# Stick-breaking prompt attention: the suffix sums from one float32 product to two products of rounded parts

## The chip, the cores and the metric

The kernel runs on one core of a Trainium2 chip. TensorE (PE in the rows, its weight loads PEld) does matrix products into the accumulation memory PSUM, VectorE (DVE) does elementwise work, ScalarE (ACT) evaluates functions such as Exp and Ln from tables that it must load first, GpSimd (POOL) and SyncE (SP) issue transfers. Each engine works through its own list of instructions in order and waits on semaphores that the others raise. The metric is the device time of one execution in microseconds (us); lower is better.

## The reference

The program is one layer of a decoder: projections, stick-breaking attention and dilated-window attention for a prompt of 512 positions and for 8 sampled sequences, an output projection, and a feed-forward part with product-key experts. The change touches one piece: the stick-breaking attention of the prompt, for 8 heads.

```python
def stick_breaking_weights(z, mask):
    log_keep = jnp.where(mask, jax.nn.log_sigmoid(-z), 0.0)
    later = lax.cumsum(log_keep, axis=z.ndim - 1, reverse=True) - log_keep
    return jnp.where(mask, jnp.exp(jax.nn.log_sigmoid(z) + later), 0.0)
...
z = jnp.einsum('bqhd,bkhd->bhqk', qi, k) * scale + b
mask = kpos[None, :] < qpos[:, None]
w = stick_breaking_weights(z, mask)
return jnp.einsum('bhqk,bkhd->bqhd', w.astype(v.dtype), v)
```

Since log_sigmoid(-z) is minus softplus(z), the weight of key s for query t is the exponential of z minus the sum of softplus(z) over the keys from s up to the query. So each head needs a suffix sum over keys of the softplus of its logits.

## The kernel before

Keys lie on the 128 partitions, in four blocks (KB = 4). Block kb has its logits for the queries from its own block on, 512, 384, 256 and 128 columns, and the four pieces stand side by side in one tile of WIDE = 1280 columns. Per head h the stage does this:

- **Scores, TensorE** (`scores`, L596 and L598): four products of keys and queries and four that add the mask, into PSUM banks 0 to 2. They wait for the logits of the head before, which empties those banks.
- **Logits, VectorE** (`logits`, L671): scale and bias, PSUM to `sb_z`, three tiles in turn.
- **Log part, ScalarE** (`log_part`, L643 to L645): Abs, Exp of its negative, Ln of one plus that, into `sb_e`; the Ln (and later the Exp again) needs a table load in front of it.
- **Softplus, VectorE** (`softplus`, L680): max(z, 0) plus the log part, into `sb_p`, two tiles in turn. It raises `sb_softplus`.
- **Sums, TensorE** (L624 and L627): for each block one product with a lower triangle of ones (`tri`) and one with a full square of ones (`ones`) for every later block, into PSUM banks 3 to 5. Ten products of 128 to 512 columns, 2560 columns together, all in float32. They raise `sb_sums`.
- **Exponents, VectorE** (L689): z minus the sums, in place in `sb_z`, raising `sb_exponents`.
- **Weights, ScalarE** (L658): Exp in place, after a table load; and `out` (L649) copies the result of the head before.
- **Weigh, TensorE** (`weigh`, L609): ten products of weights and values.

The order on each engine is written out by hand. TensorE: scores of head h+1, sums of h, weigh of h-1. ScalarE: log part of h+1, weights of h, out of h-1. VectorE: logits of h+1, exponents of h, softplus of h+1:

```python
logits(0)
softplus(0)
for h in range(H):
    if h + 1 < H:
        logits(h + 1)
    dve.wait_ge(sem("sb_sums"), h + 1)
    dve.tensor_tensor(sb_z[h % 3], sb_z[h % 3], bank(3, 3)[:, 0:WIDE], ALU.subtract)\
        .then_inc(sem("sb_exponents"), 1)
    if h + 1 < H:
        softplus(h + 1)
```

In the trace a float32 product stands as two matmul records with a weight load each. Elsewhere in the program (the projections at L405, the experts at L2065) a float32 operand is kept as two parts of type float32r, a rounded one and the rest, and the products of the parts are added; a float32r product stands as one record. `own_steps` gives an engine a counting semaphore of its own; `link` raises it on an instruction and waits for it, so that the next instruction may read what this one wrote, and `do` raises it without waiting.

The dilated-window attention (L710 to L820) follows on the same engines, and the sampled sequences come after it, behind a barrier of all engines.

Of the kernel before, what the change touches and what calls it, by code (L numbers as in the profile page):

```python
# [26 lines left out]
F32R = mybir.dt.float32r  # L27
# [3 lines left out]
ALU = mybir.AluOpType  # L31
# [3 lines left out]
P = 128  # L35
# [41 lines left out]
ALL_COLUMNS = 52992  # L77
# [88 lines left out]
def build(nc, x_prompt, x_sample, cache_k_sb, cache_v_sb, page_table, state_k_win, state_v_win,  # L166
# [4 lines left out]
    with ExitStack() as ctx:  # L171
# [20 lines left out]
        def sem(name):  # L192
            name = AGAIN.get(name, name)
            if name not in made:
                made[name] = ctx.enter_context(nc.semaphore(name))
            return made[name]
# [4 lines left out]
        def take_in(stack, name, cols):  # L201

            era_tensor[0] = stack.enter_context(nc.sbuf_tensor(name, [P, cols], F32)), cols, place[0]
# [6 lines left out]
        def take(cols, at=None):  # L210

            if at is not None:
                place[0] = at
            o = place[0]
            place[0] = o + cols
            if place[0] <= KEPT:
                return kept[:, o:o + cols]
            tensor, size, base = era_tensor[0]
            assert o >= base and place[0] <= base + size, (o, place[0], base, size)
            return tensor[:, o - base:o - base + cols]  # L220

        def bank(b, n=1):
            return psum[:, b * BANK:(b + n) * BANK]
# [4 lines left out]
        ident, tri, ones, diag, iota = (sq[:, i * P:(i + 1) * P] for i in range(5))  # L228
# [11 lines left out]
        SAMPLE = place[0]  # L240
        assert SAMPLE == KEPT + ATTENTION
        work_era = ExitStack()
# [30 lines left out]
        def part(engine):  # L273
            return programs[engine].append
        steps = {}

        def own_steps(eng, name):

            if name not in steps:
                steps[name] = Steps(eng, sem(f"{name}_step"))  # L280
            return steps[name]
# [33 lines left out]
        @part("sp")  # L315
        def _(sp):
            sp.dma_start(sq, square).then_inc(sem("square_in"), 16)
            for t in range(4):
                sp.dma_start(x_nat[:, t, :], x_rows[:, t, :]).then_inc(sem(X_IN[t]), 16)
            sp.wait_ge(sem("tail_cleared"), 1)  # L320
            sp.dma_start(x_nat[0:NS, 4, :], xs_rows).then_inc(sem("small_in"), 16)
            sp.dma_start(cos_sb, cosine).then_inc(sem("angles_in"), 16)
            sp.dma_start(sin_sb, sine).then_inc(sem("angles_in"), 16)
            sp.dma_start(pages_sb[:, :], page_table.rearrange("b j -> (b j)").rearrange("(o n) -> o n", o=1))\
              .then_inc(sem("pages_in"), 16)
            for g in range(NG_IN):
                for e in range(2):
                    if g >= 1:
                        sp.wait_ge(sem("w_low"), 2 * (g - 1) + e + 1)
                    sp.dma_start(w_sb[e], w_in_g[2 * COLUMN[GROUPS[g // 2]] + g % 2, e]).then_inc(sem(f"w_in_{e}"), 16)  # L330
# [218 lines left out]
        KB = SEQ // P  # L549
        AT = (0, 512, 1024, 896)  # L550
        WIDE = 1280
        work_era.close()
        place[0] = SAMPLE
        take_in(work_era, "prompt_attention", ALL_COLUMNS - SAMPLE)
        place[0] = WORK
        sb_z = [take(WIDE) for _ in range(3)]
        sb_e = [take(WIDE) for _ in range(2)]
        sb_p = [take(WIDE) for _ in range(2)]
        o_nat = take(4 * D).rearrange("p (t d) -> p t d", t=4)
        counts = take(4 * SEQ).rearrange("p (t k) -> p t k", t=4)  # L560
        bias = small[:, 0:8]
        bias_ht = small[:, 8:40].rearrange("p (h t) -> p h t", h=H)
# [10 lines left out]
        def region(kb):  # L573
            return slice(AT[kb], AT[kb] + SEQ - kb * P)
# [14 lines left out]
        @part("pe")  # L589
        def _(pe):  # L590
            def scores(h):
                if h >= 1:
                    pe.wait_ge(sem("sb_logits"), h)
                for kb in range(KB):
                    r = region(kb)
                    pe.matmul(psum[:, r], lhsT=k_t["sb"][:, h // 2, kb * P:(kb + 1) * P],  # L596
                              rhs=q_z["sb"][:, h, kb * P:SEQ], start=True, stop=False)
                    last = pe.matmul(psum[:, r.start:r.start + P], lhsT=ident, rhs=diag, start=False, stop=True)  # L598
                last.then_inc(sem("sb_scores"), 1)

            def weigh(h):
                pe.wait_ge(sem("sb_weights"), h + 1)
                if h >= 2:
                    pe.wait_ge(sem("sb_out_copied"), h - 1)
                out = bank(6 + h % 2)
                for qb in range(KB):
                    for kb in range(qb + 1):
                        a = AT[kb] + (qb - kb) * P
                        last = pe.matmul(out[:, qb * HD:(qb + 1) * HD], lhsT=sb_z[h % 3][:, a:a + P],  # L609
                                         rhs=v_n["sb"][:, kb, h * HD:(h + 1) * HD], start=(kb == 0), stop=(kb == qb))  # L610
                last.then_inc(sem("sb_out"), 1)


            scores(0)
            for h in range(H):
                if h + 1 < H:
                    scores(h + 1)
                pe.wait_ge(sem("sb_softplus"), h + 1)
                if h >= 1:
                    pe.wait_ge(sem("sb_exponents"), h)  # L620
                sp_h = sb_p[h % 2]
                for kb in range(KB):
                    r = region(kb)
                    last = pe.matmul(bank(3, 3)[:, r], lhsT=tri, rhs=sp_h[:, r], start=True, stop=(kb == KB - 1))  # L624
                    for later in range(kb + 1, KB):
                        a = r.start + (later - kb) * P
                        last = pe.matmul(bank(3, 3)[:, a:r.stop], lhsT=ones, rhs=sp_h[:, region(later)],  # L627
                                         start=False, stop=(later == KB - 1))
                last.then_inc(sem("sb_sums"), 1)
                if h >= 1:  # L630
                    weigh(h - 1)
            weigh(H - 1)
# [29 lines left out]

        @part("dve")
        def _(dve):
            dve.wait_ge(sem("counts_in"), 2 * 16)

            def logits(h):
                dve.wait_ge(sem("sb_scores"), h + 1)
                if h >= 3:
                    dve.wait_ge(sem("sb_out"), h - 2)  # L670
                dve.tensor_scalar(sb_z[h % 3], psum[:, 0:WIDE], SCALE, bias[:, h:h + 1], ALU.mult, ALU.add)\  # L671
                    .then_inc(sem("sb_logits"), 1)

            def softplus(h):

                dve.wait_ge(sem("sb_log"), h + 1)
                dve.wait_ge(sem("sb_logits"), h + 1)
                if h >= 2:
                    dve.wait_ge(sem("sb_sums"), h - 1)
                dve.scalar_tensor_tensor(sb_p[h % 2], sb_z[h % 3], 0.0, sb_e[h % 2], ALU.max, ALU.add)\  # L680
                    .then_inc(sem("sb_softplus"), 1)

            logits(0)
            softplus(0)
            for h in range(H):
# [7 lines that stand above are left out]
# [1673 lines left out]
```

## Time and profile before

| | us |
|---|---|
| median of 3 runs (2473.87 to 2479.03) | 2478.3 |
| the profiled execution, whole | 2474.16 |
| span of its trace | 2472.3 |
| TensorE busy | 2304.7 (93%) |
| VectorE busy | 1549.5 (63%) |
| ScalarE busy | 942.2 (38%) |
| the 8 heads of the stage, first logits to last exponents | 210.94 to 293.32 |

Busy time is the union of an engine's instructions on the span; the span starts with the first instruction that the profiler saw. The stage that the change touches takes about 82 us of the 2472.3, so a number for the whole kernel says little of it: it is read from windows and single rows of that stage.

### The profile page before, as it was taken

The page shows a single profiled execution, that of the slowest core. Times are in us where ns is not written, and L with a number is a line of the kernel's source. Part 1 is how long each engine was busy: PE and PEld are TensorE (multiplying, and loading weights), DVE is VectorE, ACT ScalarE, POOL GpSimd, SP SyncE. Part 2 cuts the span into 40 slices and gives each one's busy share as a digit, 9 for nine tenths or more (in the row PEclk, how much of TensorE's full clock was granted, in tenths as well). Part 3 has the DMA queues.
Part 4 walks back from the last instruction along what each step waited for, and adds up shares of the span by engine and source line. Part 5 has one row for each costly group of instructions (what it writes and reads, how often), then busy time and mean ns, then how long its engine had stood idle before and what let it go on. Part 6 is the DMA issues. An engine that isn't in the chain of part 4 may idle for free.

```text
span 2472.3 us, 37860 instructions
## 1 busy us (share of the span) xinstructions
PE 2304.7 (93%) x12921; PEld 1901.2 (77%) x12921; DVE 1549.5 (63%) x3167; ACT 942.2 (38%) x1432; POOL 393.3 (16%) x370
## 2 busy tenths in 40 slices
PE   7998988998999798999899889999999999999996
PEld 7997765666566446985577688999989899999895
DVE  4352331333444434678998778777777777777777
ACT  3225542444444512223355633333333333333332
POOL 0001000000000000000000044333333333333320
PEclk9999987889999898999999999999999999999998
DMA  4226977877766621203254699999999999999982
GB/s 130 87 88 224 332 237 271 275 263 263 267 207 209 196 66 37 83 21 106 92 197 178 243 333 342 317 313 315 314 313 311 316 315 311 312 313 313 311 294 78
DMA packets 224111, 568.20 MB, mean 230 GB/s; under 512 B 18065, under 2 KB 96466, under 8 KB 221330
## 3 DMA queue, kind: packets, MB, share of 16 engines
q1 hardware_dynamic: 174994, 327.75, 40.2%
q0 software_dynamic: 49024, 239.23, 27.6%
q8 instruction: 56, 0.92, 0.1%
q14 instruction: 37, 0.30, 0.0%
HBM read 528.24 MB, written 105.12 MB: 256 GB/s over the span
## 4 chain that ended last, share of the span: by engine, by line
PE 79%; DVE 8%; DMA 4%; ACT 3%; SPq 3%; issue 2%; POOL 0%; ACTq 0%; DVEq 0%
PE psum L2065 20%; PE psum L2056 16%; PE psum L405 7%; PE psum L1560 5%; PE psum L1839 5%; PE psum L2046 3%; DMA sample<-in_cache_v_sb_dram 3%; PE psum L1862 3%; PE psum L1420 3%; PE psum L1001 3%; PE psum L1055 2%; PE psum L991 2%; PE psum L1073 2%; PE psum L1023 1%; SPq L926 1%
## 5 line engine op out<-in xcount | busy, mean ns | idle before, releaser
L2065 PE MATMUL psum<-expert_parts 128*128 128x512 f32 x2304 | 550.3, 394 | 0.8 <-DVE expert_parts L2184 0.8
L2065 PEld LDWEIGHTS psum<-expert_parts 128*128 128x128 f32 x2304 | 426.7, 188 | 87.3 <-DVE expert_parts L2184 1.8
L2056 PE MATMUL psum<-h_parts,expert_parts 128*128 128x384 f32 x2304 | 444.5, 341 | 2.9 <-DVE expert_parts L2179 1.5
L2056 PEld LDWEIGHTS psum<-h_parts,expert_parts 128*128 128x128 f32 x2304 | 403.0, 189 | 10.9 <-issue 1.8
L2126 ACT ACTIVATE expert_parts<-peer 128x1024 fp32r<-128x1024 f32 x128 | 135.8, 1061 | 358.9 <-PE psum L2065 332.8
L2179 DVE TENSOR_TENSOR expert_parts<-psum,expert_parts 128x512 fp32r<-128x512 f32 x192 | 132.8, 692 | 147.2 <-ACT expert_parts L2120 147.2
L2222 DVE SCALAR_TENSOR_TENSOR kept<-experts,kept 128x1024 f32<-128x1024 f32 x160 | 205.0, 1281 | 8.3 <-DMA experts<-in_peer_v_dram,kept 3.0
L2031 POOL DMA_INDIRECT experts<-in_peer_v_dram,kept x160 | 192.6, 1204 | 70.5 <-issue 47.5
L1839 PE MATMUL psum<-h_whole,gate_table 128*128 128x384 f32 x512 | 180.6, 497 | 10.5 <-ACT gate_table L1891 10.5
L1331 DVE TENSOR_TENSOR sample_parts<-sample,sample_parts 128x512 fp32r<-128x512 f32 x128 | 85.5, 690 | 166.9 <-ACT sample_parts L1184 166.5
L405 PE MATMUL psum<-projection_parts 128*128 128x256 f32 (+1 forms) x1440 | 174.5, 283 | 3.8 <-DVE projection_parts L511 3.8
L405 PEld LDWEIGHTS psum<-projection_parts 128*128 128x128 f32 (+1 forms) x1440 | 170.6, 175 | 6.0 <-issue 3.9
L2120 ACT ACTIVATE expert_parts<-psum 128x512 fp32r<-128x512 f32 x192 | 114.8, 598 | 149.1 <-PE psum L2046 142.5
L2184 DVE TENSOR_TENSOR expert_parts<-peer,expert_parts 128x1024 fp32r<-128x1024 f32 x128 | 155.9, 1218 | 0.0
L1839 PEld LDWEIGHTS psum<-h_whole,gate_table 128*128 128x128 f32 x512 | 93.8, 193 | 67.5 <-issue 18.1
L2026 POOL DMA_INDIRECT experts<-in_peer_u_dram,kept x96 | 95.3, 992 | 314.4 <-DVE experts L2206 180.2
L1160 ACT ACTIVATE sample<-psum 128x512 f32<-128x512 f32 x128 | 75.8, 593 | 164.4 <-PE psum L991 164.4
L2026 POOL DMA_INDIRECT peer<-in_peer_u_dram,kept x62 | 79.7, 1285 | 361.9 <-DVE peer L2206 356.6
L1001 PEld LDWEIGHTS psum<-attention,sample 128*128 128x128 f32 x1024 | 134.7, 204 | 1.6 <-issue 0.8
L2046 PE MATMUL psum<-kept,peer 128*128 128x128 f32 x768 | 115.7, 273 | 16.1 <-DVE expert_parts L2179 15.7
L1001 PE MATMUL psum<-attention,sample 128*128 (+1 forms) x1024 | 130.5, 254 | 0.0
L1023 PE MATMUL psum<-sample_parts 128*64 128x512 f32 x272 | 96.4, 482 | 25.0 <-DVE sample_parts L1331 24.2
(281 smaller groups left out, 3287.1 us busy)
## 6 DMA issues: line engine op xcount, KB each, us to landing
peer<-in_peer_v_dram SPq DMA_DIRECT2D x128, 512.0 KB, 5.0
peer<-in_peer_u_dram SPq DMA_DIRECT2D x96, 512.0 KB, 5.4
sample<-in_cache_k_sb_dram SPq DMA_DIRECT2D x128, 256.0 KB, 3.9
sample<-in_cache_v_sb_dram SPq DMA_DIRECT2D x128, 256.0 KB, 3.0
out_dram<-in_state_k_win_dram POOLq DMA_DIRECT2D x8, 4088.0 KB, 54.4
out_dram<-in_state_v_win_dram POOLq DMA_DIRECT2D x8, 4088.0 KB, 41.2
gates_dram<-gate_table SPq DMA_DIRECT2D x12, 2048.0 KB, 7.3
experts<-gates_dram SPq DMA_DIRECT2D x32, 768.0 KB, 6.8
```

Of the source, the lines that this page charges most:

```text
L405: last = pe.matmul(bank(u % 4)[0:r, 0:WC], lhsT=x_r[:, x, k, t * P:t * P + r], rhs=w_in_r[g % 2][:, y, k, :], start=(n == 1), stop=(n == 3 ...
L1001: last = pe.matmul(bank(2)[:, c:c + 8].rearrange("p (e t) -> p e t", e=2), lhsT=k_turned[j % 2][:, pair, :], rhs=q_s["sb"][:, 2 * pair:2 * ...
L1839: last = pe.matmul(bank(6)[:, 0:ND], lhsT=early_t[e % 2][:, k, :], rhs=h1_f[:, k, :], start=(k == 0), stop=(k == KD - 1))
L2026: pool.indirect_dma_start(out=u_rows[p], out_offset=None, in_=peer_u, in_offset=index(q, p))\
L2031: pool.indirect_dma_start(out=v_rows[p], out_offset=None, in_=peer_v, in_offset=index(q - 1, p))\
L2046: last = pe.transpose(bank(7)[:, k % 4 * P:(k % 4 + 1) * P], u_sb[s][:, k * P:(k + 1) * P], ident)
L2056: last = pe.matmul(bank(6)[:, 0:ND], lhsT=u_t[s][:, a, k, :], rhs=h1_r[:, b, k, 0:ND], start=(k == 0 and n == 0), stop=(k == KD - 1 and n ...
L2065: last = pe.matmul(bank(2 * t + half), lhsT=weight[s][:, a, t * P:(t + 1) * P], rhs=v_r[s][:, b, half * 512:(half + 1) * 512], start=(firs ...
L2126: act.activation(v_r[s][:, 0, :], v_sb[s], ACT.Copy).then_inc(sem("v_high"), 1)
L2179: dve.tensor_tensor(u_t[s][:, 1, ks, :], bank(7).rearrange("p (k j) -> p k j", k=4), u_t[s][:, 0, ks, :], ALU.subtract).then_inc(sem("u_lo ...
L2184: dve.tensor_tensor(v_r[s][:, 1, :], v_sb[s], v_r[s][:, 0, :], ALU.subtract).then_inc(sem("v_low"), 1)
L2222: dve.scalar_tensor_tensor(y, v_rows[p], dots_act[:, p:p + 1], y, ALU.mult, ALU.add).then_inc(sem("added"), 1)
```

## The change

The softplus of a head is still made in `sb_p`, but then split on VectorE into a rounded part (`tensor_copy` into a float32r tile) and what the rounding left (`tensor_tensor` subtract). The ten products per head become twenty, in float32r, a pair of parts for each. `tri` and `ones` are copied once into float32r tiles. The order of logits, exponents and softplus on VectorE is that of before. The memory for the parts, 4 x 1280 + 2 x 128 columns, is taken from the end of the stage's area.

```diff
+        SUMS_R = 4 * WIDE + 2 * P
+        take_in(work_era, "prompt_attention", ALL_COLUMNS - SAMPLE - SUMS_R)
+        sums_tensor = work_era.enter_context(nc.sbuf_tensor("sums_parts", [P, SUMS_R], F32R))
...
+        sp_r = [sums_tensor[:, 2 * e * WIDE:2 * (e + 1) * WIDE].rearrange("p (x n) -> p x n", x=2) for e in range(2)]
+        tri_r, ones_r = (sums_tensor[:, 4 * WIDE + e * P:4 * WIDE + (e + 1) * P] for e in range(2))
...
-                sp_h = sb_p[h % 2]
                 for kb in range(KB):
                     r = region(kb)
-                    last = pe.matmul(bank(3, 3)[:, r], lhsT=tri, rhs=sp_h[:, r], start=True, stop=(kb == KB - 1))
+                    for x in range(2):
+                        last = pe.matmul(bank(3, 3)[:, r], lhsT=tri_r, rhs=sp_r[h % 2][:, x, r], start=(x == 0),
+                                         stop=(kb == KB - 1 and x == 1))
                     for later in range(kb + 1, KB):
                         a = r.start + (later - kb) * P
-                        last = pe.matmul(bank(3, 3)[:, a:r.stop], lhsT=ones, rhs=sp_h[:, region(later)],
-                                         start=False, stop=(later == KB - 1))
+                        for x in range(2):
+                            last = pe.matmul(bank(3, 3)[:, a:r.stop], lhsT=ones_r, rhs=sp_r[h % 2][:, x, region(later)],
+                                             start=False, stop=(later == KB - 1 and x == 1))
...
+            st = own_steps(dve, "dve")
             dve.wait_ge(sem("counts_in"), 2 * 16)
...
-                dve.scalar_tensor_tensor(sb_p[h % 2], sb_z[h % 3], 0.0, sb_e[h % 2], ALU.max, ALU.add)\
+                st.link(dve.scalar_tensor_tensor(sb_p[h % 2], sb_z[h % 3], 0.0, sb_e[h % 2], ALU.max, ALU.add))
+                st.link(dve.tensor_copy(sp_r[h % 2][:, 0, :], sb_p[h % 2]))
+                dve.tensor_tensor(sp_r[h % 2][:, 1, :], sb_p[h % 2], sp_r[h % 2][:, 0, :], ALU.subtract)\
                     .then_inc(sem("sb_softplus"), 1)
 
+            st.do(dve.tensor_copy(tri_r, tri))
+            st.do(dve.tensor_copy(ones_r, ones))
             logits(0)
             softplus(0)
```

VectorE at the start of the stage, before: logits of head 0, softplus of 0, logits of 1, exponents of 0, softplus of 1, logits of 2.

```order
L671 TENSOR_SCALAR prompt_attention<-psum,kept 128x1280
L680 SCALAR_TENSOR_TENSOR prompt_attention<-prompt_attention 128x1280
L671 TENSOR_SCALAR prompt_attention<-psum,kept 128x1280
L689 TENSOR_TENSOR prompt_attention<-prompt_attention,psum 128x1280
L680 SCALAR_TENSOR_TENSOR prompt_attention<-prompt_attention 128x1280
L671 TENSOR_SCALAR prompt_attention<-psum,kept 128x1280
```

VectorE at the same place in the changed kernel, whose lines are L678 for the logits, L687 to L689 for the softplus and its two parts, and L700 for the exponents; `sums_parts` is the new float32r tile, and the two 128x128 rows are the copies of `tri` and `ones`.

```order
L692 CAST sums_parts<-kept 128x128
L693 CAST sums_parts<-kept 128x128
L678 TENSOR_SCALAR prompt_attention<-psum,kept 128x1280
L687 SCALAR_TENSOR_TENSOR prompt_attention<-prompt_attention 128x1280
L688 CAST sums_parts<-prompt_attention 128x1280
L689 TENSOR_TENSOR sums_parts<-prompt_attention,sums_parts 128x1280
L678 TENSOR_SCALAR prompt_attention<-psum,kept 128x1280
L700 TENSOR_TENSOR prompt_attention<-prompt_attention,psum 128x1280
L687 SCALAR_TENSOR_TENSOR prompt_attention<-prompt_attention 128x1280
L688 CAST sums_parts<-prompt_attention 128x1280
L689 TENSOR_TENSOR sums_parts<-prompt_attention,sums_parts 128x1280
L678 TENSOR_SCALAR prompt_attention<-psum,kept 128x1280
```

Two instructions stand behind each softplus now, in front of the logits of the next head; nothing changed places.

TensorE, the sums of head 0 and the first scores behind them, before:

```order
L624 MATMUL psum<-prompt_attention,kept 128x512
L627 MATMUL psum<-prompt_attention,kept 128x384
L627 MATMUL psum<-prompt_attention,kept 128x256
L627 MATMUL psum<-prompt_attention,kept 128x128
L624 MATMUL psum<-prompt_attention,kept 128x384
L627 MATMUL psum<-prompt_attention,kept 128x256
L627 MATMUL psum<-prompt_attention,kept 128x128
L624 MATMUL psum<-prompt_attention,kept 128x256
L627 MATMUL psum<-prompt_attention,kept 128x128
L624 MATMUL psum<-prompt_attention,kept 128x128
L596 MATMUL psum<-prompt 128x512
```

TensorE at the same place in the changed kernel (L628 and L633 are the sums, L600 the scores):

```order
L628 MATMUL psum<-sums_parts 128x512 x2
L633 MATMUL psum<-sums_parts 128x384 x2
L633 MATMUL psum<-sums_parts 128x256 x2
L633 MATMUL psum<-sums_parts 128x128 x2
L628 MATMUL psum<-sums_parts 128x384 x2
L633 MATMUL psum<-sums_parts 128x256 x2
L633 MATMUL psum<-sums_parts 128x128 x2
L628 MATMUL psum<-sums_parts 128x256 x2
L633 MATMUL psum<-sums_parts 128x128 x2
L628 MATMUL psum<-sums_parts 128x128 x2
L600 MATMUL psum<-prompt 128x512
```

Each product stands twice, once for each part, in the same order.

## Rows read from the trace of the kernel before

**Rows 1.** Windows of the stage: window, its length, busy time, granted clock (1.00 is 2.4 GHz).

```profile
250.00:260.00 10.00, 10.00 (x61) 8.02 (x60) 4.53 (x3) 8.29 (x8) 0.00 (x0) 1.00 0.99 322
280.00:285.00 5.00, 3.67 (x30) 3.44 (x28) 2.53 (x2) 4.92 (x5) 0.00 (x0) 1.00 1.01 340
...
287.00:290.00 3.00, 3.00 (x8) 1.95 (x7) 0.00 (x0) 0.00 (x0) 0.00 (x0) 0.55 0.93 305
```

**Rows 2.** Chain that ended last, in the stage: start, us, what.

```profile
277.19 1.56 DVE prompt_attention L671
...
285.51 1.35 PE psum L624 x2
```

**Rows 3.** Timeline of VectorE: start, duration, instruction, idle time in front and its releaser.

```profile
210.94 1.55 DVE L671 TENSOR_SCALAR prompt_attention<-psum,kept 128x1280 f32<-128x1280 f32 x1 [27.42 <-DMA prompt_attention<-in_count_prompt_dram]
217.78 1.49 DVE L680 SCALAR_TENSOR_TENSOR prompt_attention<-prompt_attention 128x1280 f32<-128x1280 f32 x1 [5.28 <-ACT prompt_attention L645]
219.19 1.54 DVE L671 TENSOR_SCALAR prompt_attention<-psum,kept 128x1280 f32<-128x1280 f32 x1
...
235.40 1.49 DVE L680 SCALAR_TENSOR_TENSOR prompt_attention<-prompt_attention 128x1280 f32<-128x1280 f32 x1 [0.50 <-ACT prompt_attention L645]
238.70 1.55 DVE L671 TENSOR_SCALAR prompt_attention<-psum,kept 128x1280 f32<-128x1280 f32 x1 [1.81 <-PE psum L598]
...
245.47 1.49 DVE L680 SCALAR_TENSOR_TENSOR prompt_attention<-prompt_attention 128x1280 f32<-128x1280 f32 x1 [0.95 <-ACT prompt_attention L645]
248.32 1.55 DVE L671 TENSOR_SCALAR prompt_attention<-psum,kept 128x1280 f32<-128x1280 f32 x1 [1.36 <-PE psum L598]
252.66 1.49 DVE L689 TENSOR_TENSOR prompt_attention<-prompt_attention,psum 128x1280 f32<-128x1280 f32 x1 [2.79 <-PE psum L624]
...
277.19 1.55 DVE L671 TENSOR_SCALAR prompt_attention<-psum,kept 128x1280 f32<-128x1280 f32 x1 [1.36 <-PE psum L598]
...
283.96 1.49 DVE L680 SCALAR_TENSOR_TENSOR prompt_attention<-prompt_attention 128x1280 f32<-128x1280 f32 x1 [0.95 <-ACT prompt_attention L645]
291.83 1.49 DVE L689 TENSOR_TENSOR prompt_attention<-prompt_attention,psum 128x1280 f32<-128x1280 f32 x1 [6.38 <-PE psum L624]
```

**Rows 4.** Timeline of ScalarE, the end of one head's log part.

```profile
252.50 1.28 ACT L645 ACT_TABLE_LOAD   x1
253.79 1.27 ACT L645 ACTIVATE prompt_attention<-prompt_attention 128x1280 f32<-128x1280 f32 x1
```

**Rows 5.** Timeline of TensorE: first sums product of a head, its weigh.

```profile
248.12 1.02 PE L624 MATMUL psum<-prompt_attention,kept 128*128 128x512 f32 x2
...
252.46 2.34 PE L609 MATMUL psum<-attention,prompt_attention 128*128 128x64 f32 x20
```

**Rows 6.** Timeline of VectorE in the rotary embedding of the projections.

```profile
119.45 1.48 DVE L498 TENSOR_TENSOR attention<-attention,kept 128x1280 f32<-128x1280 f32 x1
120.85 1.48 DVE L499 TENSOR_TENSOR kept<-attention,kept 128x1280 f32<-128x1280 f32 x1
122.37 1.49 DVE L500 TENSOR_TENSOR attention<-attention,kept 128x1280 f32<-128x1280 f32 x1
...
128.35 0.83 DVE L504 COPY attention<-attention 128x1280 f32<-128x1280 f32 x1
```

**Rows 7.** Groups by line and shape on VectorE: casts (x count, us in all, mean ns).

```profile
L1670 DVE CAST kept<-kept 128x128 f32<-128x128 uint32 x8 | 1.5, 224 | 0.1
...
L1622 DVE CAST peer<-peer 128x512 f32<-128x512 uint32 x2 | 0.8, 422 | 0.0
```

**Rows 8.** Timeline of TensorE: runs of products of float32r parts.

```profile
99.81 4.44 PE L405 MATMUL psum<-projection_parts 128*128 128x256 f32 x36
...
1889.80 2.43 PE L2065 MATMUL psum<-expert_parts 128*128 128x512 f32 x10
```

**Rows 9.** Timeline of TensorE: scores of one head after a pause, and without one.

```profile
212.55 2.07 PE L596 MATMUL psum<-prompt 128*128 128x512 f32 x2 [5.47 <-DVE prompt_attention L671]
...
254.64 1.08 PE L596 MATMUL psum<-prompt 128*128 128x512 f32 x2
```

More of the change, by code:

```diff
@@ L553, in build @@
         place[0] = SAMPLE
-        take_in(work_era, "prompt_attention", ALL_COLUMNS - SAMPLE)
+        SUMS_R = 4 * WIDE + 2 * P
+        take_in(work_era, "prompt_attention", ALL_COLUMNS - SAMPLE - SUMS_R)
+        sums_tensor = work_era.enter_context(nc.sbuf_tensor("sums_parts", [P, SUMS_R], F32R))
         place[0] = WORK
```

## The prediction

> **What bounds the stage now.** The windows come first. In a steady piece of the stage TensorE is busy for 10.00 of 10.00 us at the full 2.4 GHz, VectorE for 4.53 and ScalarE for 8.29; only behind the last scores does TensorE fall idle, and its granted clock then drops to 0.55 [rows 1]. The chain of waits agrees: through the middle heads it is TensorE all the way, and it leaves TensorE only with the last head, at 277.19, where it runs through VectorE and ScalarE and comes back to the sums at 285.51 [rows 2]. VectorE's timeline gives the period and the slack. Logits start at 238.70 and 248.32, so a head takes 9.62 us, and in front of the logits VectorE waits 1.36 us for the scores [rows 3]; three other heads show the same 1.36.
>
> What the busy shares do not show is a loop a little shorter than TensorE's work. VectorE makes the logits of head h+1; ScalarE takes its log part from them; VectorE waits for that and makes the softplus of h+1; and only then, by its written order, does it reach the logits of h+2. Logits to softplus took 6.77 us (238.70 to 245.47, and 277.19 to 283.96 again) [rows 3]. That is three functions and a table load on ScalarE, the last two of which are shown [rows 4]; the change touches none of it. Softplus to the next logits, where nothing is waited for, took 1.41 us (217.78 to 219.19) [rows 3]. The loop is thus 6.77 + 1.41 = 8.18 us and has 1.44 us of slack under 9.62. Since softplus and logits are both in the loop, anything put between them lengthens it.
>
> **The change part by part.**
>
> *The sums.* A head's sums run from 248.12 to 252.46, 4.34 us for 2560 columns in float32 [rows 5]. Twenty float32r products have 5120 columns. Runs of such products took 4.44 us for 36 of 256 columns and 2.43 us for ten of 512 [rows 8], 0.48 ns a column at most, so 2.5 us. Products of only 128 columns in float32r are not in the trace. If each took as long as a weight load and a product of the weigh, 2.34/20 = 0.117 us [rows 5], the eight of them would make it 2.9 us; if they kept the float32 price of 4.34/2560 = 1.7 ns a column, 3.7 us. I take 2.5, because all neighbours in float32r are that fast. For the middle heads it hardly matters: TensorE's head falls from 9.62 to 7.8 us (9.62 - 4.34 + 2.5), and TensorE stops being the bound.
>
> *The split.* Two instructions of 1280 columns now stand between softplus and the next logits. The subtract is like the tensor-tensor operations of the rotary embedding, on the same 128x1280 shape: 1.48 us each and 1.40 from start to start when the second does not wait for the first, 1.52 when it does (119.45, 120.85, 122.37) [rows 6]. The rounding copy is listed as a cast. A plain copy of this shape took 0.83 us [rows 6], and casts between other 4-byte types took 224 ns at 128 columns and 422 at 512 [rows 7], which extends to 0.82 us at 1280; so I take 0.83. Were the rounding done at one element at a time, it would be 1.49, as softplus is. From softplus to the next logits it is then 1.52 (with its wait) + 0.86 (the copy and its wait, 0.03) + 1.41 = 3.79 us instead of 1.41: 2.38 us more, in every head.
>
> On the waits that `link` adds, the rows show 0.12 us each (1.52 against 1.40). The Trainium skill ("VectorE: DVE Perf Modes", The DRAIN you can't avoid) says instead that a semaphore between chained operations costs nothing extra. By it the whole sum below would be 16 x 0.12 = 1.9 us smaller; the trace does not agree, and I stay with the row.
>
> *The loop after.* 6.77 + 3.79 = 10.56 us, against 7.8 on TensorE and ScalarE's 8 us a head (8.29 busy in 10, a head 9.62) [rows 1]. So the loop becomes the bound and a middle head goes from 9.62 to 10.56. The exponents, on VectorE between logits and softplus, stay covered: sums start 0.1 us after the logits do and end 2.6 behind their start, the exponents end at about 4.2, and the softplus waits for ScalarE until 6.77. Even at half the clock (below, 4.7 us for the sums) they end at 6.4.
>
> *Summed over the heads.* The logits of heads 1 to 7 each come behind a split, 7 x 2.38 = 16.7 us. Those of heads 1 and 2 waited for nothing, so their share is paid in full. Those of heads 3 to 7 had slack: 3.30 - 1.41 = 1.89 (235.40 to 238.70) and four times 1.44 [rows 3], 7.65 together. That leaves 9.0. The copies of `tri` and `ones` stand in front of the first logits, whose input had just landed (idle 27.42 us, released by a transfer) [rows 3], so they are paid too: two of 224 ns [rows 7], 0.4. The logits of head 7 start 9.4 us later than 277.19. Behind them comes the eighth split: the sums of head 7 started 1.55 us behind the softplus (283.96 to 285.51) [rows 2, 3], and will start 1.52 + 0.86 + 1.55 = 3.93 behind it. They are 11.8 us late.
>
> *The last sums* are on the path alone. Before they took 6.3 us (285.51 to 291.83) [rows 2, 3] instead of 4.34, because TensorE had paused and the clock was at 0.55 [rows 1]. Now TensorE pauses longer: it is through with the sums of head 6 and the weigh at 286.6 + 2.5 + 2.3 = 291.4 and gets the last softplus at 297.3, 5.9 us later. A pause of 5.47 us at 212.55 left it at half speed, 2.07 us for what took 1.08 [rows 9]. So the last sums take 2.5 x 1.92, about 4.7 us; 1.6 come back (3.8 if the clock stays full at 2.5; with slow narrow products at half clock, 7.1, nothing, and 0.8 is lost). What follows in the stage is the same work in the same order, and the sampled sequences begin behind a barrier, so the delay reaches the end whole.
>
> **The sum.** 9.4 + 2.4 - 1.6 = +10.2 us. The profiled execution took 2474.16, which gives 2484.4; it stands 4.1 us under the median of the runs, 2478.3. For the median I forecast 2478.3 + 10.2 = 2488.5 us, +0.4%. A measurement of this kernel tells about 0.2%, 5 us, from no change.
>
> **The rivals.**
>
> *TensorE stays the bound, and the change gains.* If the split were hidden, a head would be ScalarE's 8 us in place of 9.62, and over five heads 8 us would go: 2470. Busy shares speak for it, since TensorE is at 10.00 of 10.00 and VectorE at 4.53 [rows 1]. Against it stands the loop. It turns at 1.44 us of added VectorE time in a head; even with a subtract as fast as the copy, 0.83, the split adds 1.7. Chance 0.04.
>
> *The rounding copy runs at one element at a time.* 0.66 us more in each of eight splits, 5.3 us: +15.5, 2494. The casts [rows 7] speak against it, but none of them makes float32r. Chance 0.06.
>
> *The clock falls in every head.* TensorE will now pause about 2.8 us per head. The pause before the last sums, some 1.8 us (1.33 idle us in the window up to 285 and 0.51 more), was followed by a clock of 0.55, and the one of 5.47 by half speed [rows 1, 2, 9]. A burst of sums, weigh and scores wholly at half speed would take 15.6 us instead of 7.8 and be the bound, +5 in each of six heads. Half of that, since the clock rises again in steady work, is +15: 2503. It decides once a burst needs more than 10.56 us, that is, once more than 2.8 us are lost to the clock in a head. This is what the Trainium skill warns of ("TensorE: Matmul & The Clock Gate", HAM oscillation): pauses between bursts can bring the throttle back burst after burst. The trace agrees as far as these two single pauses go; a pause that comes back head after head is not in this stage. Chance 0.08.
>
> *Part is paid back.* The last sums at full clock (2.5 us, +8.0), and the first products of the dilated heads, which stand behind them, at a better clock than now by another 3 us or more: +5 or less, 2480 to 2483, not to be told from no change. I know of nothing that would wake TensorE there. Chance 0.10.
>
> **The numbers.** My forecast has 0.72, with 2484 to 2493 as its own range (last sums from 2.5 to 7.1 us, and a few tenths in each head's waits). The range 2479 to 2500 takes in the slow copy, the payback and the spread of the runs, and leaves out most of the clock rival and the gain. Slower by over 0.2%: 0.72 + 0.06 + 0.08 = 0.86; within it 0.10; faster 0.04.
>
> **What would show it.** Logits 10.56 us apart in the middle heads, with no wait in front of them; softplus, cast and subtract back to back, the cast near 0.83; TensorE idle for some 2.8 us before each head's sums, released by VectorE's subtract; the sums 2.5 us in the middle heads; last exponents near 302. Wrong it would be if logits still waited for scores (TensorE the bound), or if the granted clock sat low through the stage.

## The result

The changed kernel took 2487.35 us in the median of 14 runs (2479.99 to 2495.22); the kernel before, run beside it, took 2474.72 (14 runs, 2465.99 to 2487.14). The ratio is 1.0046, with a 95% interval of 1.0029 to 1.0063: 7 to 16 us slower. The forecast was +10.2 us, 0.41%, and slower.

VectorE's timeline of the changed kernel shows the loop (start, duration, instruction, idle time in front and its releaser):

```profile
234.46 1.55 DVE L678 TENSOR_SCALAR prompt_attention<-psum,kept 128x1280 f32<-128x1280 f32 x1
...
247.85 1.55 DVE L678 TENSOR_SCALAR prompt_attention<-psum,kept 128x1280 f32<-128x1280 f32 x1 [2.75 <-PE psum L602]
...
254.63 1.49 DVE L687 SCALAR_TENSOR_TENSOR prompt_attention<-prompt_attention 128x1280 f32<-128x1280 f32 x1 [2.57 <-ACT prompt_attention L651]
256.15 0.83 DVE L688 CAST sums_parts<-prompt_attention 128x1280 fp32r<-128x1280 f32 x1
257.02 1.49 DVE L689 TENSOR_TENSOR sums_parts<-prompt_attention,sums_parts 128x1280 fp32r<-128x1280 f32 x1
258.42 1.55 DVE L678 TENSOR_SCALAR prompt_attention<-psum,kept 128x1280 f32<-128x1280 f32 x1
...
282.38 1.55 DVE L678 TENSOR_SCALAR prompt_attention<-psum,kept 128x1280 f32<-128x1280 f32 x1
...
292.94 1.54 DVE L678 TENSOR_SCALAR prompt_attention<-psum,kept 128x1280 f32<-128x1280 f32 x1
...
308.46 1.49 DVE L700 TENSOR_TENSOR prompt_attention<-prompt_attention,psum 128x1280 f32<-128x1280 f32 x1 [4.87 <-PE psum L628]
```

Against [rows 3]: the wait in front of the logits is gone in most heads. Softplus, cast and subtract stand back to back, and the next logits follow 3.79 us behind the softplus (254.63 to 258.42). Where nothing else interferes a head takes 10.56 us (282.38 to 292.94), in place of 9.62. In two heads the logits came 13.39 us apart (234.46 to 247.85, and once more behind 258.42), and there they did wait for the scores. The windows of the same execution say why (window, length, busy times, granted clock):

```profile
240.00:250.00 10.00, 10.00 (x49) 8.39 (x49) 5.82 (x5) 4.58 (x5) 0.00 (x0) 0.69 0.92 307
...
260.00:270.00 10.00, 10.00 (x39) 8.66 (x39) 5.30 (x4) 7.92 (x7) 0.00 (x0) 0.50 0.93 314
270.00:280.00 10.00, 9.82 (x68) 8.57 (x66) 4.46 (x3) 6.52 (x6) 0.00 (x0) 1.00 1.02 334
```

TensorE is busy throughout two of these windows, but at 0.50 and, as the mean of a window in which it rose, 0.69 of its clock, where a steady stretch before had 1.00 [rows 1]. Its timeline shows the pause ahead of the fall, a head at full speed, and the last sums:

```profile
258.56 0.73 PE L628 MATMUL psum<-sums_parts 128*128 128x512 f32 x2 [2.70 <-DVE sums_parts L689]
...
262.75 4.47 PE L613 MATMUL psum<-attention,prompt_attention 128*128 128x64 f32 x20
...
293.08 0.74 PE L628 MATMUL psum<-sums_parts 128*128 128x512 f32 x2 [0.65 <-DVE sums_parts L689]
...
295.52 0.34 PE L633 MATMUL psum<-sums_parts 128*128 128x128 f32 x2
...
295.91 2.39 PE L613 MATMUL psum<-attention,prompt_attention 128*128 128x64 f32 x20
...
303.65 1.22 PE L628 MATMUL psum<-sums_parts 128*128 128x512 f32 x2 [5.34 <-DVE sums_parts L689]
```

A pause of 2.70 us ends at 258.56; the weigh behind it takes 4.47 us where it takes 2.39 at full clock. After such a slow head TensorE was late and began the next sums without a pause (247.57 and 271.53), at full clock, so that in this execution the clock fell in the sums of every second head, 1, 3, 5 and 7. In head 5 it was up again when the weigh began (2.56 us), and the logits lost nothing. At full clock the sums take 2.83 us (293.08 to 295.91) instead of 4.34 [rows 5], and the last sums, behind a pause of 5.34, take 4.81 (303.65 to 308.46) instead of 6.32. The last exponents start at 308.46, 16.6 us later than the 291.83 of before [rows 3]; 0.8 us of it is that the stage began later in this execution, because its first transfer landed later.

### The profile page after: what moved, and what is told of

It reads as the page before. It is cut to its first block, busy times and chain, and to the rows that moved or that the text cites. A ratio compares the mean times of both kernels' runs of the same rounds, so it can differ in the third digit from the quotient of the medians.

```text
span 2484.5 us, 37878 instructions
## 1 busy us (share of the span) xinstructions
PE 2302.0 (93%) x12921; PEld 1908.3 (77%) x12921; DVE 1568.2 (63%) x3185; ACT 942.8 (38%) x1432; POOL 394.6 (16%) x370
## 4 chain that ended last, share of the span: by engine, by line
PE 78%; DVE 9%; DMA 4%; ACT 3%; SPq 3%; issue 2%; POOL 0%; ACTq 0%; DVEq 0%
PE psum L2076 20%; PE psum L2067 16%; PE psum L405 7%; PE psum L1571 5%; PE psum L1850 5%; PE psum L2057 3%; PE psum L1873 3%; DMA sample<-in_cache_v_sb_dram 3%; PE psum L1012 3%; PE psum L1431 3%; PE psum L1066 2%; PE psum L1002 2%; PE psum L1084 2%; PE psum L1034 1%; SPq L937 1%
```

## The experiments

Three theories stood against each other. A: the split lengthens the loop from logits over log part, softplus and split to the next logits past TensorE's work, and the clock that falls in TensorE's pauses costs a second part. B: the split is hidden, and the shorter products leave pauses whose falling clock is the cost. D: whatever stands behind a softplus costs its whole time, slack or no slack.

They were timed in two groups of four, each group against the kernel before on one chip. Runs of one kernel scatter by some 10 us either way, as much as the whole effect, so the intervals reach some 0.2 to 0.4% either way, and the stage is read from the profiles. There is one profile of each kernel, and two of the changed one.

### The split alone

```diff
-                    for x in range(2):
-                        last = pe.matmul(bank(3, 3)[:, r], lhsT=tri_r, rhs=sp_r[h % 2][:, x, r], start=(x == 0),
-                                         stop=(kb == KB - 1 and x == 1))
+                    last = pe.matmul(bank(3, 3)[:, r], lhsT=tri, rhs=sp_h[:, r], start=True, stop=(kb == KB - 1))
```

(The same for `ones`; `sp_h` is again `sb_p[h % 2]`.)

> The split on VectorE stays, but the sums are the ten float32 products of before, on the unsplit softplus; the two parts are made and not used. Theory A (the split lengthens the loop logits, log part, softplus, split, next logits): logits 10.56 us apart in the middle heads, TensorE pausing only about 0.9 us a head and its clock at 1.00, about +12 us over the kernel before, 2487. Rival B (the split is hidden, and it is the pauses that the shorter products make on TensorE, with the clock falling in them, that cost the time): no clock falls, at most the one split before the last sums shows, about +2 us, 2477.

2490.07 us (6 runs), ratio 1.0080 (1.0049 to 1.0112). VectorE's logits, the last exponents, and a window:

```profile
244.72 1.55 DVE L676 TENSOR_SCALAR prompt_attention<-psum,kept 128x1280 f32<-128x1280 f32 x1
...
255.28 1.54 DVE L676 TENSOR_SCALAR prompt_attention<-psum,kept 128x1280 f32<-128x1280 f32 x1
...
304.50 1.49 DVE L698 TENSOR_TENSOR prompt_attention<-prompt_attention,psum 128x1280 f32<-128x1280 f32 x1 [6.89 <-PE psum L628]
```

```profile
250.00:260.00 10.00, 9.33 (x53) 7.18 (x53) 6.26 (x5) 7.36 (x8) 0.00 (x0) 1.00 1.00 329
```

The heads take 10.56 us with the float32 products too, at a clock of 1.00, with no fall between the second and the last head. The last exponents start 12.7 us late. So the split costs time by itself, and rival B falls: it needs shorter products, and there are none here. The run also settles rival D: 2.38 us more stand behind each softplus, and with TensorE's products those of before a head grew by 0.94 (9.62 to 10.56), the 2.38 less the 1.44 of slack.

### The products alone

```diff
-                st.link(dve.scalar_tensor_tensor(sb_p[h % 2], sb_z[h % 3], 0.0, sb_e[h % 2], ALU.max, ALU.add))
-                st.link(dve.tensor_copy(sp_r[h % 2][:, 0, :], sb_p[h % 2]))
-                dve.tensor_tensor(sp_r[h % 2][:, 1, :], sb_p[h % 2], sp_r[h % 2][:, 0, :], ALU.subtract)\
+                dve.scalar_tensor_tensor(sp_r[h % 2][:, 0, :], sb_z[h % 3], 0.0, sb_e[h % 2], ALU.max, ALU.add)\
```

(And both products of a pair read part 0 in place of part `x`.)

> No split: softplus is written straight into the rounded tile and both products of a pair read it, so the sums are twice those of the rounded softplus. VectorE's list is that of before. Theory A: the loop is 8.2 us, TensorE's work 7.9 and ScalarE's 8.0, so logits come 8.2 to 8.5 us apart instead of 9.62; about -8 us against the kernel before, 2467, some of it lost if the clock falls behind the shorter pauses. Rival B: pauses on TensorE with falling clock, so no gain or slower, 2475 to 2485.

2471.47 us (12 runs), ratio 0.9999 (0.9976 to 1.0021): no gain to be told. VectorE's logits, then TensorE behind the pause and a window:

```profile
229.62 1.55 DVE L678 TENSOR_SCALAR prompt_attention<-psum,kept 128x1280 f32<-128x1280 f32 x1
...
244.31 1.55 DVE L678 TENSOR_SCALAR prompt_attention<-psum,kept 128x1280 f32<-128x1280 f32 x1 [6.25 <-PE psum L602]
...
252.49 1.54 DVE L678 TENSOR_SCALAR prompt_attention<-psum,kept 128x1280 f32<-128x1280 f32 x1
...
261.00 1.55 DVE L678 TENSOR_SCALAR prompt_attention<-psum,kept 128x1280 f32<-128x1280 f32 x1 [0.25 <-PE psum L602]
```

```profile
229.75 1.22 PE L628 MATMUL psum<-sums_parts 128*128 128x512 f32 x2 [3.37 <-DVE sums_parts L687]
```

```profile
230.00:240.00 10.00, 10.00 (x41) 9.44 (x42) 4.05 (x3) 8.78 (x8) 0.00 (x0) 0.50 0.98 321
```

The middle heads come 8.18 and 8.51 us apart, as theory A had it. But one head takes 14.69 (229.62 to 244.31), with the clock at 0.50 behind a pause of 3.4 us, and the stage ends only 0.7 us earlier than before (last exponents at 291.13). So in this execution the gain was there, and the clock took most of it back in a single head. My -8 us left that out. That the timed runs lost it in the same way is not shown: only one of them was profiled.

### The logits ahead of the split

```diff
+                    if h + 2 < H:
+                        logits(h + 2)
+                    split(h + 1)
```

(`softplus` ends behind its first instruction; `split` holds the cast and the subtract. `logits(1)` and `split(0)` stand ahead of the loop.)

> The changed kernel with VectorE's order turned: softplus of head h+1, logits of h+2, and only then the cast and the subtract of h+1. Nothing is left out. Theory A: the split leaves ScalarE's loop (8.2 us), but another loop comes up: softplus, logits, cast, subtract, sums, exponents, softplus = 1.41 + 1.47 + 0.86 + 1.55 + 2.85 + 1.41 = 9.55 us a head; 8 to 12 us under the changed kernel, about as fast as before, 2474 to 2479. Rival B: TensorE pauses as before the turn, the clock falls as often, and the time stays within 3 us of the changed kernel, 2487.

2501.24 us (6 runs), ratio 1.0140 (1.0098 to 1.0182): a miss of 25 us. VectorE through one head:

```profile
270.99 1.49 DVE L704 TENSOR_TENSOR prompt_attention<-prompt_attention,psum 128x1280 f32<-128x1280 f32 x1 [4.65 <-PE psum L628]
272.40 1.48 DVE L687 SCALAR_TENSOR_TENSOR prompt_attention<-prompt_attention 128x1280 f32<-128x1280 f32 x1
276.33 1.55 DVE L678 TENSOR_SCALAR prompt_attention<-psum,kept 128x1280 f32<-128x1280 f32 x1 [2.45 <-PE psum L602]
277.80 0.82 DVE L692 CAST sums_parts<-prompt_attention 128x1280 fp32r<-128x1280 f32 x1
278.65 1.49 DVE L693 TENSOR_TENSOR sums_parts<-prompt_attention,sums_parts 128x1280 fp32r<-128x1280 f32 x1
284.78 1.49 DVE L704 TENSOR_TENSOR prompt_attention<-prompt_attention,psum 128x1280 f32<-128x1280 f32 x1 [4.64 <-PE psum L628]
```

ScalarE no longer holds up the softplus (no wait at 272.40), so the split is out of its loop. The loop that I had counted had the wrong members. TensorE's order is sums, weigh, scores, so the logits of h+2 wait for all three (2.45 us, released by the scores' L602), and only behind them come cast and subtract, for which the next sums wait. From exponents to logits it is 5.34 us (weigh and scores), to the start of the sums 3.86 more, and the sums take 4.59, at a clock that falls behind every pause (2.83 us at full clock): 13.79 us. What VectorE takes earlier, another engine must have finished earlier.

### The pauses filled

```diff
+                if h >= 3:
+                    pe.wait_ge(sem("sb_out_copied"), h - 2)
+                for _ in range(5 if h + 1 < H else 12):
+                    pe.matmul(bank(6 + (h + 1) % 2)[:, 256:512], lhsT=ident, rhs=sq[:, 0:256], start=True, stop=True)
                 pe.wait_ge(sem("sb_softplus"), h + 1)
```

> The changed kernel with products on constants in TensorE's pauses, five float32 products of 256 columns (2.2 us) in front of each head's sums and twelve in front of the last, into unused columns of a bank. Theory A with the clock as a second cost: clock 1.00 through the stage, logits 10.56 us apart in all middle heads where the changed kernel has two of 13.39, last sums 2.8 instead of 4.8; 5 to 8 us under the changed kernel, 2480, and still about 5 us over the kernel before, which is the loop alone. If the clock costs nothing, the time stays at 2487. If it is the whole cost (rival B), it falls to that of before, 2475.

2479.13 us (11 runs), ratio 1.0043 (1.0020 to 1.0066). VectorE, the start of the last sums on TensorE, and a window:

```profile
254.72 1.55 DVE L682 TENSOR_SCALAR prompt_attention<-psum,kept 128x1280 f32<-128x1280 f32 x1
...
265.29 1.55 DVE L682 TENSOR_SCALAR prompt_attention<-psum,kept 128x1280 f32<-128x1280 f32 x1
...
300.15 1.49 DVE L704 TENSOR_TENSOR prompt_attention<-prompt_attention,psum 128x1280 f32<-128x1280 f32 x1 [3.08 <-PE psum L632]
```

```profile
297.12 0.73 PE L632 MATMUL psum<-sums_parts 128*128 128x512 f32 x2
```

```profile
260.00:270.00 10.00, 9.92 (x63) 8.43 (x63) 6.76 (x5) 7.36 (x8) 0.00 (x0) 1.00 1.07 353
```

With the clock held at 1.00 every middle head takes 10.57 us, and the last sums start 11.6 us later than before (297.12 against 285.51 [rows 2]): that is the loop by itself, without the clock. The last sums then take 3.03 us (297.12 to 300.15) instead of 6.32, so the last exponents start only 8.3 us later. Of the 3.3 us between, the kernel before had lost 2.0 to the clock (6.32 against 4.34 in a middle head); the rest is the shorter products. Against the first profile of the changed kernel the last exponents start 8.3 us earlier as well. The timed runs cannot tell the two apart (1.0020 to 1.0066 against 1.0029 to 1.0063).

### The cast alone

```diff
-                dve.tensor_tensor(sp_r[h % 2][:, 1, :], sb_p[h % 2], sp_r[h % 2][:, 0, :], ALU.subtract)\
-                    .then_inc(sem("sb_softplus"), 1)
```

(The cast raises `sb_softplus` instead, and both products of a pair read part 0.)

> The changed kernel without the subtract: both products of a pair read the rounded part, so the sums are twice those of the rounded softplus. Theory A: softplus, cast, next logits take 1.52 + 0.75 = 2.27 us instead of 1.41, which is less than the 1.44 us of slack more, so the loop is 9.04 us and shorter than the 9.62 of before: logits 9.04 apart, except where the clock falls in TensorE's pauses of about 1 us (11 to 14 there, as in the run with the products alone). Stage about as long as before or up to 3 us shorter, the whole 2470 to 2475; 12 us under the changed kernel. Rival D (any operation behind softplus costs its whole time): +7 us over before, 2480.

2473.94 us (12 runs), ratio 1.0012 (0.9995 to 1.0029). VectorE:

```profile
247.65 1.49 DVE L687 SCALAR_TENSOR_TENSOR prompt_attention<-prompt_attention 128x1280 f32<-128x1280 f32 x1 [2.57 <-ACT prompt_attention L651]
249.18 0.83 DVE L688 CAST sums_parts<-prompt_attention 128x1280 fp32r<-128x1280 f32 x1
249.92 1.54 DVE L678 TENSOR_SCALAR prompt_attention<-psum,kept 128x1280 f32<-128x1280 f32 x1
...
258.96 1.55 DVE L678 TENSOR_SCALAR prompt_attention<-psum,kept 128x1280 f32<-128x1280 f32 x1
```

9.04 us a head, as worked out, and under the 9.62 of before. But the run does not show that an operation under the slack costs nothing. With the short products TensorE no longer sets the pace: without the cast a head took 8.18 us (products alone), with it 8.18 + 0.86 = 9.04, so the cast cost its whole time. Against the kernel before, the cast and the gain of the products come together. Rival D's 2480 lies at the upper end of the interval (1.0029 times 2473); its 9.62 + 0.86 = 10.48 us a head did not come, but it had left out that the products are shorter too. What tells D from A is the split alone.

### Two passes, and the last pause filled

```diff
+        sb_z = [take(WIDE) for _ in range(4)]
...
+                for x, blocks in ((0, (0, 1, 2)), (1, (0, 1, 2)), (0, (3,)), (1, (3,))):
+                    if x == 1:
+                        pe.wait_ge(sem("sb_softplus"), h + 1)
...
+                if h + 2 < H:
+                    scores(h + 2)
                 if h >= 1:
                     weigh(h - 1)
```

> All of the computation, in another order: VectorE takes logits of head h+2 between softplus and cast of h+1; TensorE takes the scores of h+2 right behind the sums of h, ahead of the weigh of h-1, and the sums in two passes, first all products of the rounded part for three blocks, for which only the cast is waited for, then those of the rest; four tiles for the logits instead of three. This cuts the loop that turned up with the logits first (sums, weigh, scores, logits, cast, subtract, sums) to sums, scores, logits, cast, sums: 3.0 + 1.5 + 0.9 + 1.5 + 1.4 = 8.4 us; ScalarE's loop is 8.18, TensorE's work 8.0. Logits 8.4 to 8.6 us apart, TensorE hardly pausing and its clock at 1.00 from head 2 on; about 6 us under the kernel before, 2468. If the clock still falls in single heads, as with the products alone, it comes out at 2474.

2469.80 us (12 runs), ratio 0.9986 (0.9965 to 1.0006): 15 to 20 us under the changed kernel (0.9986 against 1.0046 and 1.0066), but not to be told from the kernel before. VectorE's logits:

```profile
251.44 1.54 DVE L680 TENSOR_SCALAR prompt_attention<-psum,kept 128x1280 f32<-128x1280 f32 x1
...
260.16 1.55 DVE L680 TENSOR_SCALAR prompt_attention<-psum,kept 128x1280 f32<-128x1280 f32 x1
...
269.20 1.55 DVE L680 TENSOR_SCALAR prompt_attention<-psum,kept 128x1280 f32<-128x1280 f32 x1
```

The middle heads take 8.72 and 9.04 us, the shortest with the whole computation, at a clock of 1.00. The first three heads give it back: with the scores behind the sums, and the clock at 0.66 to 0.71 there, the logits of head 3 start at 242.39, 3.7 us later than before [rows 3]; the last exponents start at 292.56, 0.7 us later than before. So the 6 us that I expected to gain were missed in the stage of this execution, although the median came near 2468: the clock was not at 1.00 from head 2 on, but at 0.71 from 230 to 240.

> As two_passes, with twelve float32 products on constants in the pause before the last sums (5.2 us, into unused columns), which keep the clock up there: last sums 2.9 us instead of 4.7. 1 to 3 us under two_passes, 2466.

2474.65 us (12 runs), ratio 1.0009 (0.9989 to 1.0029): nothing gained. The last sums do run at full clock, but the twelve products held TensorE until 290.9, some 2.7 us past the end of the cast that the sums wait for, and the last exponents start at 294.00.

### The changed kernel again

No edit.

> The changed kernel once more, for a second profile of its clock. Theory A with the clock as a second cost: logits 10.56 us apart where the clock is up, 13.4 where it fell; the number of such heads (two in the first profile) may differ, and the end of the stage with it. Time 2487 as before.

2487.46 us (6 runs), ratio 1.0066 (1.0044 to 1.0088). In this execution no middle head was slow. VectorE, then TensorE:

```profile
233.22 1.55 DVE L678 TENSOR_SCALAR prompt_attention<-psum,kept 128x1280 f32<-128x1280 f32 x1
...
243.78 1.55 DVE L678 TENSOR_SCALAR prompt_attention<-psum,kept 128x1280 f32<-128x1280 f32 x1
...
286.05 1.54 DVE L678 TENSOR_SCALAR prompt_attention<-psum,kept 128x1280 f32<-128x1280 f32 x1
...
301.91 1.49 DVE L700 TENSOR_TENSOR prompt_attention<-prompt_attention,psum 128x1280 f32<-128x1280 f32 x1 [5.21 <-PE psum L628]
```

```profile
275.62 0.73 PE L628 MATMUL psum<-sums_parts 128*128 128x512 f32 x2 [2.24 <-DVE sums_parts L689]
...
286.19 0.73 PE L628 MATMUL psum<-sums_parts 128*128 128x512 f32 x2 [2.24 <-DVE sums_parts L689]
...
290.05 4.47 PE L613 MATMUL psum<-attention,prompt_attention 128*128 128x64 f32 x20
296.75 1.22 PE L628 MATMUL psum<-sums_parts 128*128 128x512 f32 x2 [2.23 <-DVE sums_parts L689]
```

From 233.22 on the logits come 10.56 us apart and the last exponents start at 301.91, 10.1 us later than before. The clock fell here too, but later: a pause of 2.24 us left it at 1.00 in head 5 (275.62), and one just as long was followed by a fall in head 6 (286.19): the weigh behind it took 4.47 us. No scores stand behind that weigh, so no logits waited for it; the last sums took 5.16 us (296.75 to 301.91). The number of middle heads that the clock lengthens differs from execution to execution: two in the first profile, none here.

## Why the prediction held

The delay of the last exponents against the kernel before, taken apart in the three profiles in which the whole split stands behind the softplus (us, each rounded by itself; the eighth split counts to the start of the last sums):

| | forecast | first profile | second profile | pauses filled |
|---|---|---|---|---|
| start of the stage | - | +0.8 | -0.5 | -0.1 |
| copies of `tri` and `ones` | +0.4 | +0.3 | +0.3 | +0.3 |
| loop, heads 1 to 7 | +9.0 | +9.0 | +9.0 | +9.0 |
| middle heads with a slow clock | - | +5.7 | - | - |
| eighth split | +2.4 | +2.4 | +2.4 | +2.4 |
| last sums | -1.6 | -1.5 | -1.2 | -3.3 |
| sum | +10.2 | +16.6 | +10.1 | +8.3 |

- **The loop.** Right to the hundredth: 3.79 us from softplus to the next logits, 10.56 us a head, and 9.0 us over the heads in each of the three profiles. The split alone shows it with the old products, and the filled pauses with a clock of 1.00. The turning point at 1.44 us of slack was not tried by itself; it is borne out by the split alone, where 2.38 us more cost 0.94 a head.
- **The cast** took 0.83 us, so the rival of a slow copy is out. The two copies of `tri` and `ones` took 0.28 us, not 0.4.
- **The sums.** 2.83 us at full clock, not 2.5. The bound of 2.9 was nearer, though not for its reason: products of 128 columns took 0.085 us each, not 0.117. The pause in front of a head's sums was 2.24 us where the clock stayed up, not 2.8. As said, this was hidden in the middle heads.
- **The last sums.** 4.81 us in the first profile and 5.16 in the second, against 4.7. The pause in front of them was 5.34 us, against 5.9, in the first; in the second it was 2.23, because the clock had fallen a head earlier.
- **The clock rival** was underrated as a part and overrated as a whole. It does not come in every head, at +15 us; it lengthened two heads of one execution, 2.83 us each, and no middle head of another. The case that was left out of the list is the one between: the loop in every head, and the clock in some.
- **Part is paid back** did not happen in the stage: the last sums were slow in both profiles. Behind it, some did in the first profile. The clock was up there when the dilated heads began, and from the last weigh to their third group of products it took 10.84 us (311.31 to 322.15), where it had taken 14.20 before (294.68 to 308.88), 3.4 us less. In the second profile the clock was down there, and nothing came back.

The first products of the dilated heads, before and in the first profile of the changed kernel:

```profile
297.34 3.65 PE L710 MATMUL psum<-prompt 128*128 128x128 f32 x8
...
313.59 2.38 PE L721 MATMUL psum<-prompt 128*128 128x128 f32 x8
```

Farther behind, the kernels differ although their work is the same. Against the kernel before, the changed one was 16.6 us late at the last exponents and 12.2 in its span, its second profile 10.1 and 12.9, the filled pauses 8.3 and 2.6. A large step of it can be read: in the part on the sampled sequences the same work ran at a clock of 0.62 before and at 1.00 in the first profile of the changed kernel, which gains 4.9 us on the way (and so do the filled pauses, at 1.00 too; the second profile, at 0.63, does not). The two windows, before and after:

```profile
400.00:410.00 10.00, 10.00 (x57) 9.29 (x57) 1.78 (x7) 3.31 (x6) 0.00 (x0) 0.62 1.08 420
...
414.60:424.60 10.00, 10.00 (x75) 7.83 (x74) 1.78 (x7) 3.91 (x7) 0.00 (x0) 1.00 1.06 411
```

So that the total came out near the forecast is in part luck. In the profile first taken the stage lost 6.4 us more than forecast, most of it to two slow heads, and got 4.4 us back behind it, where the sum had put nothing. The 2488.5 us themselves stood on a median of three runs, 3.6 us above that of the kernel before run beside the changed one.

What stays open is how much of the median's 11 us (7 to 16) is the loop and how much the clock. In the three profiles the loop, with the copies and the eighth split, costs 11.7 us each time; the last sums give back 1.2 to 3.3 of it, more the higher the clock stands there, and slow heads added 5.7 in one execution. The timed runs are too wide to weigh these.

## What to carry to other kernels

An engine that is busy 45% of the time may stand in a loop that is only a little shorter than the bound. Before work goes to the idle engine to relieve the busy one, take from the timeline what lies between two of its starts on every engine and write the loops down with their lengths; the slack of the second longest, here 1.44 us a head, is all that may be spent, and it is gone as soon as the longest gets shorter: behind the shorter products even the cast alone cost its whole 0.86 us. The order in which the loops are closed must be written down for each engine: a turned order planned without one of them left this kernel at 1.0140 of the kernel before. And a gain on TensorE that turns into a pause can be lost to the clock in one head, as in the profile of the products alone.

## What the runs showed of the hardware

- In the first profile of the changed kernel, pauses of 2.83, 2.70 and 2.70 us (before 234.60, 258.56 and 282.52) were each followed by a fall of TensorE's clock, and not at once: two products of 512 columns still took 0.73 us at 258.56, and the same pair of 384 columns took 0.95 us at 259.98 that took 0.56 at full clock (294.42). In its second profile pauses of 2.24 to 2.25 us came back head after head (before 254.49, 265.05 and 275.62) with the clock at 1.00 from 250 to 280, and the next one, of 2.24 us before 286.19, was followed by a fall. So the length of the pause alone does not tell. What sets off the fall was not tried.
- With the pauses filled by products on constants the granted clock stayed at 1.00 through the middle heads, in the one execution profiled.
- Float32r products of 128 columns took 0.17 us a pair at full clock (295.52 to 295.69), 0.085 each; the pair of 512 columns took 0.58 (293.08 to 293.66).
- The rounding copy from float32 to float32r of 128x1280 took 0.83 us, the time of a plain copy [rows 6].
- Where the next instruction waited for the one before, it started 0.11 to 0.13 us later: softplus to the cast 1.52 us (254.63 to 256.15) against 1.41 to the logits, which do not wait [rows 3]; the cast to the subtract 0.87 us (256.15 to 257.02) against 0.74 to the logits (249.18 to 249.92, the cast alone).
